# Shift and scale rows of the conditioning in one PSUM bank, two columns by one product, and other banks and split positions around them

## The reference, cut to what matters

```python
c_act = jax.nn.silu(c)
for layer in range(DEPTH):
    ada = jnp.einsum('bd,de->be', c_act, w_ada[layer]) + b_ada[layer]
    shift, scale, gate = jnp.split(ada, 3, axis=-1)
    h = rms_norm(x, norm_g[layer]) * (1.0 + scale[:, None, :]) + shift[:, None, :]
    y = even_mixer(h, ...) if layer % 2 == 0 else odd_mixer(h, ...)
    x = x + gate[:, None, :] * y
```

## Time and profile before

| | us |
|---|---|
| three runs, median (lowest to highest) | 803.86 (803.84 to 804.42) |
| the profiled execution's own time | 801.96 |
| span of its profile | 800.2 |
| PE busy | 757.0 (95%) |
| DVE busy | 500.0 (62%) |
| ACT busy | 379.0 (47%) |

### The profile page before, as it was taken

How to read it: one execution, slowest core, us unless ns; L and a number is a source line. 1 busy time by engine, 2 the same in 40 slices (tenths; PEclk the granted TensorE clock), 3 DMA queues, 4 the chain that set the end, 5 groups by cost and what they waited for, 6 DMA issues and landing times.

```text
span 800.2 us, 12225 instructions
## 1 busy us (share of the span) xinstructions
PE 757.0 (95%) x5042; PEld 646.7 (81%) x5042; DVE 500.0 (62%) x679; ACT 379.0 (47%) x571; POOL 26.6 (3%) x40
## 2 busy tenths in 40 slices
PE   4889999999899899996999999999999999999998
PEld 2577786468688678684899999999887999999886
DVE  1384767745865755777458999955867554455441
ACT  2464565644344546652453335389545534344320
POOL 3100000100000000001200000000000000000000
PEclk9899999999999999998999999999999999999999
DMA  9983546652447326324274455551535454544611
GB/s 368 377 332 143 213 158 276 262 227 67 170 161 286 133 85 231 110 102 168 104 264 158 163 209 177 192 184 48 196 125 211 157 177 194 211 175 149 251 58 52
DMA packets 21830, 146.50 MB, mean 183 GB/s; under 512 B 2496, under 2 KB 2656, under 8 KB 5264
## 3 DMA queue, kind: packets, MB, share of 16 engines
q1 hardware_dynamic: 20736, 142.32, 47.6%
q0 software_dynamic: 768, 2.37, 0.9%
q10 hardware_dynamic: 272, 1.05, 0.3%
HBM read 144.68 MB, written 1.05 MB: 182 GB/s over the span
## 4 chain that ended last, share of the span: by engine, by line
PE 79%; DVE 8%; ACT 5%; issue 4%; DMA 3%; POOL 1%; POOLq 0%; DVEq 0%; ACTq 0%
PE banks L438 22%; PE banks L439 22%; PE banks L440 22%; DVE WL L1598 4%; PE banks L522 3%; PE banks L544 2%; DMA ROTS<-in_weights_dram 1%; PE banks L607 1%; ACT WH L1120 1%; PE banks L646 1%; PE banks L559 1%; ACT PROBS L1222 1%; DMA CST<-in_consts_dram 1%; PE banks L614 1%; ACT PROBS L1220 1%
## 5 line engine op out<-in xcount | busy, mean ns | idle before, releaser
L1598 DVE TENSOR_TENSOR WL<-RAW,WH 128x2048 fp32r<-128x2048 f32 x107 | 242.9, 2280 | 81.0 <-ACT WH L1120 80.5
L1120 ACT ACTIVATE WH<-RAW 128x2048 fp32r<-128x2048 f32 x107 | 203.3, 1905 | 99.1 <-PE banks L440 71.8
L438 PE MATMUL banks<-HH,WH 128*128 128x256 f32 x768 | 218.5, 285 | 0.5 <-DVE WL L1598 0.5
L439 PE MATMUL banks<-HL,WH 128*128 128x256 f32 x768 | 217.8, 284 | 0.0
L440 PE MATMUL banks<-HH,WL 128*128 128x256 f32 x768 | 217.8, 284 | 0.0
L438 PE MATMUL banks<-WH,HH 128*128 128x512 f32 (+1 forms) x336 | 136.4, 406 | 17.2 <-DVE HL L1657 5.4
L438 PEld LDWEIGHTS banks<-HH,WH 128*128 128x128 f32 x768 | 148.0, 193 | 1.2 <-DVE WL L1598 1.1
L439 PEld LDWEIGHTS banks<-HL,WH 128*128 128x128 f32 x768 | 147.9, 193 | 0.1
L440 PEld LDWEIGHTS banks<-HH,WL 128*128 128x128 f32 x768 | 147.9, 193 | 0.0
L439 PE MATMUL banks<-WL,HH 128*128 128x512 f32 (+1 forms) x336 | 132.7, 395 | 0.0
L440 PE MATMUL banks<-WH,HL 128*128 128x512 f32 (+1 forms) x336 | 132.7, 395 | 0.0
(11 more groups left out here) (273 smaller groups left out, 862.0 us busy)
## 6 DMA issues: line engine op xcount, KB each, us to landing
RAW<-in_weights_dram SPq DMA_DIRECT2D x114, 1024.0 KB, 4.9
BIG<-in_weights_dram SPq DMA_DIRECT2D x6, 1024.0 KB, 7.5
ROTS<-in_weights_dram SPq DMA_DIRECT2D x4, 1024.0 KB, 8.9
PROBS<-in_weights_dram SPq DMA_DIRECT2D x2, 1024.0 KB, 9.4
RAW<-in_weights_dram SPq DMA_DIRECT2D x2, 816.0 KB, 7.4
GATE<-in_weights_dram SPq DMA_DIRECT2D x3, 512.0 KB, 8.0
X<-in_x_dram ACTq DMA_DIRECT2D x1, 1024.0 KB, 5.9
QT<-in_weights_dram SPq DMA_DIRECT2D x1, 1024.0 KB, 13.7
```

Source lines behind the costliest of these rows:

```text
L438: pe.matmul(out_, lhsT=w[0], rhs=x[0], start=start, stop=False, **more)
L439: pe.matmul(out_, lhsT=w[0], rhs=x[1], start=False, stop=False, **more)
L1120: do(act.activation(WH[:, s % SPLIT_RING, 0:kb * width], RAW[:, slot[n] % RAW_RING, 0:kb * width], ACT.Copy), high_done)
L1598: do(dve.tensor_tensor(WL[:, s % SPLIT_RING, w], RAW[:, slot[n] % RAW_RING, w], WH[:, s % SPLIT_RING, w], ALU.subtract), low_done)
```

## The change

**Conditioning.** `CACT` becomes 33 columns per block with the value in column 1 and zeros elsewhere. Columns 1 to 32 put the value's products on partition 0 of each group of 32, columns 0 to 31 on partition 1. So shift (c = 0, 1) goes to row 0 and scale (c = 2, 3) to row 1 of the same bank, in one accumulation, and there are two banks and two `row_in` of a layer where there were four. `SEL` is a tile of two columns, made by one `tensor_reduce` of the identity once it has landed; one product with it gives the shift column and the scale column of 128 features, written eight columns apart. The bias comes by two DMAs, not one. In layer 0 both halves of c = 2 run before the first columns.

**Other banks.** `q1_0`, `k1_0`, `q2` and `k2` at t = 1 open a bank of `out` in place of `proj`, and `gate_rows(1)` opens `score`.

**Other places.** `norm_turn(1, 1)` stands ahead of all of `k1_0` at t = 0. `compressed_scores` stands behind `weigh(1)`. `highs` and `lows` change places in both attentions: in layer 0 splits 11 to 15 are made in steps 2 to 5 (they were in 2, 3, 4 and, the last, 6 on ACT and 7 on DVE), in layer 1 `rotate` of `k1_1` and the splits around it are one step later on DVE, and ACT's `highs` go ahead of the evictions in each step. On ACT `head_turn("qb", 0)` goes ahead of `gate_half("za.0", 0)`. DVE's product of `MIXR` and `FING` moves from behind `add_output(1, 0, 1)` into step 9. Around `output`, DVE makes split 17 behind `low_tile` and `add_output(0, 1, 0)`, and split 37 ahead of `add_output(1, 1, 1)`, split 38 ahead of `stat_twice(1)`.

```diff
@@ -190,11 +190,11 @@
-        QUADS = sb("QUADS", [P, P])
+        QUADS, SEL = sb("QUADS", [P, P]), sb("SEL", [P, 2])
...
-        CACT, CTMP = sb("CACT", [P, KB]), sb("CTMP", [P, KB])
+        CACT, CTMP = sb("CACT", [P, KB, 33]), sb("CTMP", [P, KB])
@@ -536,14 +536,16 @@
-                use, name = f"cols{layer}.{c}", f"ada{layer}_{c}"
-                bank = tiles[ps.uses[use][0]] if half else ps.open(pe, kind, use)
+                row, name = (c // 2, f"ada{layer}_{c}") if c < 4 else (0, f"ada{layer}_{c}")
+                use = f"cols{layer}.{c % 2 if c < 4 else c}"
+                first, last = half == 0 and row == 0, half == 1 and (c >= 4 or row == 1)
+                bank = ps.open(pe, kind, use) if first else tiles[ps.uses[use][0]]
...
-                    mm = pe.matmul(bank[32 * k:32 * k + 32, :], lhsT=CACT[:, kk:kk + 1].to_broadcast([P, 32]),
-                                   rhs=raw_block(name, half, k), start=(half == 0), stop=(half == 1))
-                if half:
+                    mm = pe.matmul(bank[32 * k:32 * k + 32, :], lhsT=CACT[:, kk, 1 - row:33 - row],
+                                   rhs=raw_block(name, half, k), start=first, stop=last)
+                if last:
@@ -556,8 +558,8 @@
-                    mm = pe.matmul(bank[:, j:j + 1], lhsT=ACC[:, j * P:(j + 1) * P], rhs=QUADS[:, 0:1],
-                                   start=True, stop=True)
+                    mm = pe.matmul(bank[:, 0:2 * KB].rearrange("p (u b) -> p u b", u=2)[:, :, j],
+                                   lhsT=ACC[:, j * P:(j + 1) * P], rhs=SEL[:, :], start=True, stop=True)
@@ -570,8 +572,9 @@
+                pe.wait_ge(quads_set, 4)
...
-                    bank = ps.open(pe, "proj", f"gate{layer}.{c}")
+                    bank = ps.open(pe, ("proj", "score")[layer], f"gate{layer}.{c}")
@@ -674,6 +677,8 @@
+                    for what in after.get(i - a, ()):
+                        what()
@@ -756,12 +761,11 @@
-            conditioning_half(0, 2, 0, "out")
-            pe.wait_ge(quads_set, 4)
+            conditioning_half(0, 2, 0)
+            conditioning_half(0, 2, 1)
+            pe.wait_ge(sel_set, 1)
...
-            columns_of(first_columns, 0, 0)
-            conditioning_half(0, 2, 1)
-            ps.fill(columns_of(first_columns, 0, 2), "ada0.0")
+            ps.fill(columns_of(first_columns, 0, 0), "ada0.0")
@@ -770,8 +774,8 @@
-            conditioning_row(0, 3, "out")
-            conditioning(0, "ada0.1", (1, 3), "out")
+            conditioning_row(0, 3)
+            conditioning(0, "ada0.1", (1,), "out")
@@ -799,25 +803,25 @@
-                          3: [lambda: by_features("zb", 0), compressed_scores], 4: [lambda: conditioning_row(0, 4)],
+                          3: [lambda: by_features("zb", 0)], 4: [lambda: conditioning_row(0, 4)],
...
-                          12: [lambda: conditioning(1, "ada1", (0, 1, 2, 3), "out")],
-                          13: [lambda: half_tokens("wo0_1", 0, 0, use="y0.0.1", heads=0)]})
+                          12: [lambda: conditioning(1, "ada1", (0, 1), "out")],
+                          13: [lambda: half_tokens("wo0_1", 0, 0, use="y0.0.1", heads=0)]},
+                      {3: [compressed_scores]})
...
-            half_tokens("k1_0", 0, 0)
...
-            half_tokens("k1_0", 1, 0)
+            by_tokens("k1_0", 0)
...
-            by_tokens("q1_0", 1)
+            by_tokens("q1_0", 1, kind="out")
...
-            by_tokens("k1_0", 1)
+            by_tokens("k1_0", 1, kind="out")
@@ -849,9 +853,9 @@
-            by_tokens("q2", 1, norm=2)
+            by_tokens("q2", 1, norm=2, kind="out")
...
-            by_tokens("k2", 1)
+            by_tokens("k2", 1, kind="out")
@@ -1051,9 +1055,13 @@
+            def bias_rows(layer):
+                pool.dma_start(ACC[0:2, 0:D], bada_in[layer, 0:2 * D].rearrange("(r d) -> r d", r=2)).then_inc(bias_in, 16)
+                pool.dma_start(ACC[0:1, 2 * D:3 * D], bada_in[layer:layer + 1, 2 * D:3 * D]).then_inc(bias_in, 16)
+
...
-            pool.dma_start(ACC[0:1, :], bada_in[0:1, :]).then_inc(bias_in, 16)
+            bias_rows(0)
@@ -1329,16 +1337,16 @@
-                          1: [lambda: gate_half("za.0", 0), lambda: head_turn("qb", 0), lambda: highs(11)],
...
-                          5: [lambda: gate_half("zb.1", 3), lambda: evict("cmpT", CPT[:, :, :], flat2)],
...
+                          1: [lambda: head_turn("qb", 0), lambda: gate_half("za.0", 0), lambda: highs(11)],
...
+                          5: [lambda: highs(16), lambda: gate_half("zb.1", 3), lambda: evict("cmpT", CPT[:, :, :], flat2)],
...
-            highs(first_split("q1_0") + 2)
+            highs(first_split("q1_0") + 1)
@@ -1368,14 +1376,15 @@
...
-                          2: [lambda: head_turn("k1_1", 0), lambda: highs(odd_first + 14)],
...
+                          2: [lambda: highs(odd_first + 14), lambda: head_turn("k1_1", 0)],
...
@@ -1848,24 +1857,25 @@
+            do(dve.memset(CACT[:, :, :], 0.0), cact_half)
...
-            do(dve.scalar_tensor_tensor(CACT[:, :], CACT[:, :], 1.0, CTMP[:, :], ALU.add, ALU.mult), cact_ready)
+            do(dve.scalar_tensor_tensor(CACT[:, :, 1], CACT[:, :, 1], 1.0, CTMP[:, :], ALU.add, ALU.mult), cact_ready)
...
+            dve.wait_ge(ident_in, 16)
+            do(dve.tensor_reduce(SEL[:, :], ident.rearrange("p (g c) -> p c g", g=4)[:, 0:2, :], AX.X, ALU.add), sel_set)
...
-            row_in(0, 2)
...
-            row_in(0, 3)
@@ -1932,11 +1942,11 @@
...
-                          3: [lambda: gate(1), lambda: lows(14), compressed_mask],
...
+                          3: [lambda: gate(1), lambda: lows(13), compressed_mask],
...
+                          5: [lambda: lows(15), lambda: row_in(0, 5), lambda: lows(16)], 6: [lambda: gate(3)],
...
@@ -1945,9 +1955,9 @@
-            lows(odd_first + 2)
...
+            lows(odd_first + 2)
@@ -1961,29 +1971,32 @@
+            def scaled_rows():
+                dve.wait_ge(mixr_in, 16)
+                dve.wait_ge(fing_in, 16)
+                do(dve.tensor_tensor(MIXR, MIXR, FING[:, :], ALU.mult))
+
...
-                          1: [lambda: rotate("q1_1", 1), lambda: lows(odd_first + 12), lambda: rotate("k1_1", 0),
-                              lambda: lows(odd_first + 13)],
-                          2: [lambda: rotate("k1_1", 1), lambda: lows(odd_first + 14)],
...
+                          1: [lambda: rotate("q1_1", 1), lambda: lows(odd_first + 12)],
+                          2: [lambda: rotate("k1_1", 0), lambda: lows(odd_first + 13)],
...
-            dve.wait_ge(mixr_in, 16)
-            do(dve.tensor_tensor(MIXR, MIXR, FING[:, :], ALU.mult))
-            do.after()
...
+            lows(mix_first + 2)
...
-            lows(mix_first + 2)
+            lows(mix_first + 3)
...

```

More of the change, by code:

```diff
@@ L445, in mark_read, with by_tokens @@
                 readers[index[(name, half)]] = (piece_read, reads[0])
-            def by_tokens(name, t, width=512, use=None, norm=None):
+            def by_tokens(name, t, width=512, use=None, norm=None, kind="proj"):
                 use = use or f"{name}.{t}"
-                bank = ps.open(pe, "proj", use)
+                bank = ps.open(pe, kind, use)
                 for half in range(2):
@@ L661, in second_half, with attention @@
                     ps.wait_drained(pe, use)
-            def attention(layer, extra):
+            def attention(layer, extra, after={}):
                 a, b = spans[layer]
@@ L1070, in _ @@
                     pool.dma_start(SINK[:, :], sinks_in.partition_broadcast(P)).then_inc(sinks_got, 16)
-                    ps.wait_filled(pool, "cols0.3")
+                    ps.wait_filled(pool, "cols0.1")
                     pool.memset(CP[:, :, :, :], 0.0).then_inc(consts_set, 1)
@@ L1078, in _ @@
                     pool.wait_ge(acc_clear, 2)
-                    pool.dma_start(ACC[0:1, :], bada_in[1:2, :]).then_inc(bias_in, 16)
-                    ps.wait_filled(pool, "cols1.3")
+                    bias_rows(1)
+                    ps.wait_filled(pool, "cols1.1")
                     pool.dma_start(FING[:, :], finalg_in.partition_broadcast(P)).then_inc(fing_in, 16)
@@ L1260, in _ @@
             act.dma_start(X[:, :, :], x_in[0].rearrange("(t p) d -> p t d", t=NT)).then_inc(x_got, 16)
-            act.wait_ge(cact_half, 1)
-            do(act.activation(CACT[:, :], CTMP[:, :], ACT.Tanh), cact_tanh)
+            act.wait_ge(cact_half, 2)
+            do(act.activation(CACT[:, :, 1], CTMP[:, :], ACT.Tanh), cact_tanh)
             act.wait_ge(x_got, 16)
@@ L1640, in row_in @@
                 bank = ps.wait_filled(dve, use)
-                dve.wait_ge(bias_in, 16 * (layer + 1))
+                dve.wait_ge(bias_in, 32 * (layer + 1))
                 acc = ACC[:, c * 512:(c + 1) * 512]
@@ L1934, in _ @@
                               lambda: rotate("qb", 0), lambda: lows(10)],
-                          1: [lambda: gate(0), lambda: rotate("qb", 1), lambda: lows(11)], 2: [lambda: lows(13)],
```

(9 more changed lines are left out.)

32 lines of the change are left out of this document (17 added, 15 removed).

## The result

| | before | changed |
|---|---|---|
| median (lowest to highest) | 803.85 us (803.84 to 804.42, 4 runs) | 783.5 us (781.85 to 785.37, 4 runs) |
| the profiled execution, its span | 801.96, 800.2 | 781.85, 780.1 |
| mean granted clock of that execution | 0.980 | 0.996 |

The ratio is 0.9746 (95% interval 0.9723 to 0.9768): 20.35 us faster, where 21.5 had been forecast (782.4, range 778 to 794). In the profiled pair the difference is 20.1.

A forecast was written before the change was run, and what follows sets the result against it. PE was taken as the bound, busy 757 of 800.2 us. Terms 0.1 + 2.9 + 3.5 + 1.0 + 5.1 + 1.6 + 7.3 = 21.5 us off the 803.86 median gave 782.4, range 778 to 794.

The forecast's parts named there:

- step 5: Layer 1's attention: 2.13 us wait and low clock go, 5.1 us (bounds 2.1, 5.1); `GATE` wait, 1.6 more.
- step 1: Start: fewer column products against a later identity DMA, 0.1 us gained, bounds -0.6 and 0.4.
- step 2: Layer 0's attention: bank wait, its low clock and two DMA waits shrink or go, 2.9 us, bounds 0 and 6.
- step 3: Layer 1's columns: 8 of 16 products stay, 1.8 us, and the clock behind them holds, 1.7 more.
- C: Rival: the strided two-column write costs as much as two products; 1.8 us not won, 784.2 us; chance 0.05.
- Step 4: Start of layer 1: waits of 1.02 and 2.20 go, a new 2.1 comes; net 1.0 us, bounds 0 and 1.5.
- step 6: `q2` and `k2`: waits of 2.35 and 4.75 go, new ones come, clock gains 3.5; 7.3 us, bounds 2 and 9.
- A: Rival: the clock falls all the same, at new waits or small products; 8.2 us not won, 790.6 us; chance 0.23.
- B: Rival: moved splits ahead of `peaks` at three places of layer 0 cost 6.9 us, 789.3 us; chance 0.15.
- D: Rival: slower than before, PE staying at 0.5 clock after the wait ahead of `norm_turn(1, 1)`; 23.1 us lost; chance 0.03.
- E: Rival: the banks of `out` are themselves not free; given next to nothing, within B.

The follow-up runs named there:

- the four orders: Changed kernel with identity DMA first, `norm_turn(1, 1)` between the halves of `k1_0`, `za.0` gate before `qb`, first `val` split earlier on DVE: 777.17 us, 0.9678.
- the six products: The four orders plus six unread PE products in the wait behind the first columns: 777.65 us, ratio 0.9691.

## Why the prediction was right, and where it was not

**The sum** was 21.5, the pair of traces says 20.1. Steps 3 to 6 are within 0.4 us each. Two terms lie outside their bounds: the first by 0.8, and step 5 by 0.2 on the other side (5.30, upper bound 5.1). That the total is so near is in part luck, since step 1 and half of the parts of step 2 came out otherwise, and some 9 us of it are a clock that differs between executions.

**Step 1, the start**, was forecast at 0.1, bounds down to -0.6, and measures -1.42 in the pair. The first product comes at 24.68 for 24.07, and behind it the low stretch lasts longer. But the pair is not enough here. The turn of 54.16 stands at 56.47 in the trace with only the banks changed, whose start is the same as before. In the six traces with the changed start and nothing in the wait it stands at 54.28 to 56.09, mean 54.96. So a loss at the turn is not shown, and 1.42 is mostly these two executions. What is shown is the delay of the identity. POOL issues its DMA 0.56 later:

```profile
5.69 0.57 POOL L1063 DMA_DIRECT2D CST<-in_consts_dram  x1
...
6.25 0.57 POOL L1071 DMA_DIRECT2D CST<-in_consts_dram  x1
```

PE's first turns wait for it 0.98 to 1.46 us in the seven traces with the changed start, at 11.80 to 12.39, where it was 0.22 to 0.81 in three, at 11.31 to 11.75. The forecast had counted this delay, with the 0.66 us of the first bias DMA. With the identity first the wait goes, and the turn that this paragraph compares comes at 53.74 and, with the four orders, 53.60, sooner than in any of the six.

**Step 2**, 2.9 against 2.27, was right in its sum and wrong in its parts (those that the prediction lists, 0.2 + 2.6 + 0.3, add up to 3.1, not 2.9). The bank wait of the earlier trace rows went, but ACT's swap of `gate_half` and `head_turn` put a wait of 1.47 for `ZS` at 108.86, which I had not seen, for 0.82 won at `QT` (1.18 to 0.36); with the swap undone (the four moved orders) there is no wait for `ZS` and `QT`'s is 1.17 again. At the turn of 143.11 the lead was -2.40, 1.0 worse than at the start, where I had 0.2 better; half of that is a longer wait for a `WL` at 84.68 that other executions do not have. The DMA waits going made up for it with 3.3 to the turn of 166.54. That this is due to the moved split is not shown: with all splits in their old places 1.7 of 2.6 us went as well.

**Steps 3 and C.** 16 entries in 1.84 us: the two-column product costs what one column did, and C falls. With 32 entries the clock falls behind them in 4 of 4 traces, with 16 in 2 of 10.

**Step 4.** The new wait is 2.33, forecast 2.1; its net 1.05 for 1.0.

**Steps 5 and 6.** The waits went as forecast; the new ones ahead of `k2`, its second half and `val` are 1.54, 0.58 and 1.01 (1.3, 0.9, 1.1 forecast). The banks and layer 1's places have runs of their own; the moved splits of layer 0 and those around `q2` have none, and what they give is read from the pair alone.

**The clock and A.** I took three low stretches as the price of three waits. The count over the fourteen traces (before, changed, and the twelve above) says that they are chances:

| what precedes | traces with a low stretch behind it / traces that have it |
|---|---|
| wait of 3.4 to 4.4 at the start | 10 / 10 |
| the same with products in it that end inside | 0 / 3 |
| wait of 4.75 ahead of `q2` | 2 / 2 |
| wait of 2.34 for split 37 | 2 / 3 |
| wait of 2.13 ahead of turns, layer 1 | 3 / 4 |
| wait of 2.20 ahead of `q1_0` | 1 / 3 |
| wait of 2.33 ahead of `norm_turn(1, 1)` | 1 / 7 |
| wait of 1.65, then 32 entries of 15 columns | 3 / 4 |
| wait of 1.47 for `ZS` | 2 / 7 |
| column products, 32 entries | 4 / 4 |
| column products, 16 entries | 2 / 10 |
| wait of 1.54 in `k2` | 0 / 10 |

Apart from the last microseconds of a trace, only two more low stretches stand at other places: in the kernel of the four moved orders at 40, behind a wait of 0.90 and eight column entries, and at 19 under the six products. In the pair of traces the clock is 1.60 in step 3, 5.30 - 2.13 = 3.2 in step 5, 1.4 in step 2, and in step 6 7.71 less the waits, 7.10 - 1.54 - 0.58 - 1.01 = 3.97, so 3.7; less the 0.8 lost at the start 9.1 of the 20.1, where I had 9.6 with step 2's 1.4.

So A (the clock falls at the new waits) did not come, but it could: the clock falls behind the changed kernel's own waits in some executions, and the executions from 780.2 to 785.4 us go with mean clocks from 0.998 to 0.989. The Trainium skill, TensorE: Matmul & The Clock Gate, HAM oscillation, has idle gaps throw the array back to the lower clock. These traces agree for the long ones, 12 of 12 behind unfilled waits of some 3.4 us and more. The kernel of that section waits longer for its DMAs than the 2.1, 1.3 and 0.9 us of A, so it did not make A as likely as I wrote. For waits of 1.5 to 2.4 us the counts above decide: the clock fell behind 12 of 38, from 3 of 4 at two places to none of 10 at another. Why the places differ is open. My 8.2 us for the clock were near the truth, as far as these traces tell, because the kernel before meets many such places in each execution (its mean clock was 0.976 to 0.989 in all), and the changed one few (0.989 to 0.998).

**B** did not come. Of the waits at 128.11 and 140.64, the first (0.84 for `PROBS`) stands at 128.59 in the trace with only the banks changed too, where no split is moved, and the second (0.93) is for ACT. **D** and **E** did not come.
